# Product with the values ahead of the turn in each attention step, in a two-block transformer kernel

## What is computed

```python
sc = jnp.einsum('bnqgrd,bnkgd->bgrnqk', qb, kk).astype(jnp.float32) * (HEAD_DIM ** -0.5)
sc = jnp.where(mask, sc, NEG)
mx = jnp.maximum(sc.max(axis=-1, keepdims=True), sink)
e = jnp.exp(sc - mx)
p = e / (e.sum(axis=-1, keepdims=True) + jnp.exp(sink - mx))
o = jnp.einsum('bgrnqk,bnkgd->bnqgrd', p.astype(vv.dtype), vv)
```

## Time and profile before

| | us |
|---|---|
| median of 3 runs | 2529.38 |
| lowest and highest | 2527.14, 2529.92 |
| the profiled execution | 2531.64 |
| its span | 2529.8 |

### The profile page before, as it was taken

The page is one execution under the profiler, slowest core; times in us unless marked ns, Lnnn a source line. Parts: engine busy times, 40 slices in busy tenths (PEclk is TensorE's granted clock), DMA queues, the critical chain, the costliest instruction groups (busy, mean ns, idle before and its releaser), DMA issues.

```text
span 2529.8 us, 30118 instructions
## 1 busy us (share of the span) xinstructions
PE 2370.3 (94%) x11732; PEld 1867.3 (74%) x11732; DVE 1318.5 (52%) x1529; ACT 957.7 (38%) x1392; POOL 280.9 (11%) x188
## 2 busy tenths in 40 slices
PE   7999999999998989999998999999996689999997
PEld 6775667888876667888886678888875547788886
DVE  6447656664545656664647653333365565443333
ACT  3327753442322543442423533232225353332221
POOL 0000003110112003110100032110040001311010
PEclk9999999999999999999998999999998789999998
DMA  4211002222222002222232022322221101222231
GB/s 174 100 67 34 2 18 83 100 99 86 97 98 94 34 34 85 98 99 100 83 110 99 34 83 90 110 91 92 100 86 56 50 1 67 84 100 98 87 114 67
DMA packets 31202, 202.53 MB, mean 80 GB/s; under 512 B 4356, under 2 KB 5256, under 8 KB 7432
## 3 DMA queue, kind: packets, MB, share of 16 engines
q1 hardware_dynamic: 29816, 198.14, 22.2%
q10 hardware_dynamic: 1296, 3.15, 0.3%
HBM read 199.17 MB, written 2.10 MB: 80 GB/s over the span
## 4 chain that ended last, share of the span: by engine, by line
PE 83%; DVE 11%; ACT 4%; issue 1%; DMA 0%; ACTq 0%; DVEq 0%; SPq 0%
PE D L526 71%; PE X L600 3%; PE D L621 2%; PE D L613 2%; DVE neg_max L1680 2%; DVE w_lo L1475 1%; DVE xg L1509 1%; ACT prob L1177 1%; PE X L605 1%; ACT w_hi L1003 1%; DVE mid L1475 1%; DVE prob L1695 1%; ACT mid L1003 1%; PE X L717 1%; PE X L566 1%
## 5 line engine op out<-in xcount | busy, mean ns | idle before, releaser
L526 PE MATMUL D<-xg,w_hi 128*128 128x512 f32 x3184 | 1000.3, 396 | 57.1 <-DVE xg L1509 33.7
L526 PEld LDWEIGHTS D<-xg,w_hi 128*128 128x128 f32 x3184 | 604.4, 191 | 191.0 <-DVE w_lo L1475 25.7
L526 PE MATMUL D<-mid,w_hi 128*128 128x512 f32 x2312 | 719.2, 392 | 15.8 <-DVE w_lo L1475 7.7
L1475 DVE TENSOR_TENSOR w_lo<-w_raw,w_hi 128x2048 fp32r<-128x2048 f32 (+1 forms) x208 | 454.2, 2185 | 375.2 <-ACT w_hi L1003 374.9
L526 PE MATMUL D<-xg,w_lo 128*128 128x512 f32 x1592 | 626.3, 393 | 0.0
L1003 ACT ACTIVATE w_hi<-w_raw 128x2048 fp32r<-128x2048 f32 (+1 forms) x208 | 356.5, 1714 | 476.5 <-PE D L526 474.7
L526 PEld LDWEIGHTS D<-mid,w_hi 128*128 128x128 f32 x2312 | 436.3, 189 | 112.8 <-issue 17.6
L526 PE MATMUL D<-mid,w_lo 128*128 128x512 f32 x1156 | 452.2, 391 | 0.0
L526 PEld LDWEIGHTS D<-xg,w_lo 128*128 128x128 f32 x1592 | 303.3, 190 | 64.1
L526 PEld LDWEIGHTS D<-mid,w_lo 128*128 128x128 f32 x1156 | 218.7, 189 | 45.9
L1524 DVE TENSOR_TENSOR h<-D,h 128x1024 f32 (+1 forms) x72 | 88.0, 1222 | 267.8 <-PE D L526 267.8
(11 more groups left out here) (241 smaller groups left out, 1711.6 us busy)
## 6 DMA issues: line engine op xcount, KB each, us to landing
w_raw<-in_weights SPq DMA_DIRECT2D x184, 1024.0 KB, 4.8
h<-in_x SPq DMA_DIRECT2D x4, 512.0 KB, 7.9
out_y<-h SPq DMA_DIRECT2D x4, 512.0 KB, 2.7
inv_cnt<-in_inv_cnt ACTq DMA_DIRECT2D x1, 1024.0 KB, 4.9
cos<-in_cos ACTq DMA_DIRECT2D x3, 256.0 KB, 4.9
sin<-in_sin ACTq DMA_DIRECT2D x3, 256.0 KB, 5.3
vec<-in_vec SPq DMA_DIRECT2D x1, 262.0 KB, 3.0
cos<-in_cos_m ACTq DMA_DIRECT2D x1, 256.0 KB, 2.9
```

Source lines behind the costliest of these rows:

```text
L526: last = nc.tensor.matmul(out, w[a], x[b], start=start and k == 0, stop=stop and k == 2)
L1475: return nc.vector.tensor_tensor(out, x, f(high), ALU.subtract)
```

## The change

In TensorE's `attend` the block of the product (unit s-3) is moved ahead of the block of the turn (unit s-2). Both keep their waits: the product waits for the copy of its own unit, the turn for the norm of its own unit and for the copy of the unit before, which the product has now already waited for. In nsa the compressed product moves with the product. The two turns of the compressed branch stay where they were, before both.

```diff
-                    if 0 <= s - 2 < count:
-                        n = s - 2
-                        pe.wait_ge(normed, a0 + n + 1)
-                        if n >= 1:
-
-                            pe.wait_ge(evac, a0 + n)
...
-                        turn(kind, units[n], a0 + n)
                     if 0 <= s - 3 < count:
                         n = s - 3
                         t = n // per
...
                         pe.wait_ge(evac, a0 + n + 1)
                         times_values(kind, units[n], a0 + n, n % per == per - 1)
+                    if 0 <= s - 2 < count:
+                        n = s - 2
+                        pe.wait_ge(normed, a0 + n + 1)
+                        if n >= 1:
+
+                            pe.wait_ge(evac, a0 + n)
...
+                        turn(kind, units[n], a0 + n)
```

More of the change, by code:

```diff
@@ L685, in attend @@
                         compressed_turn(g, D[:, 3, :])
+                    if 0 <= s - 3 < count:
+                        n = s - 3
+                        t = n // per
+                        if n % per == 0:
+                            if t >= 2:
+                                pe.wait_ge(ao_low, tiles_before[l] + t - 1)
+                            if kind == "nsa":
+                                pe.wait_ge(c_evac, 4 if t % 2 else t // 2 + 1)
+                                compressed_values(t)
+                        pe.wait_ge(evac, a0 + n + 1)
+                        times_values(kind, units[n], a0 + n, n % per == per - 1)
                     if 0 <= s - 2 < count:
@@ L699, in attend @@
                         turn(kind, units[n], a0 + n)
[L700 to L711, removed]
             def swap(u, out):
```

## The result

| | before | after |
|---|---|---|
| median, us | 2529.65 (4 runs) | 2559.39 (4 runs) |
| lowest and highest | 2527.14, 2531.88 | 2554.65, 2563.93 |
| the profiled execution | 2531.64 | 2558.12 |
| its span | 2529.8 | 2556.3 |

The ratio is 1.0118, 95% interval 1.0103 to 1.0133. The changed kernel is slower, as forecast, but by 29.7 us where I had 10.0, and outside my range (2532.5 to 2546.0).

A forecast was written before the change was run, and what follows sets the result against it. TensorE was taken to set the pace in nsa and odd, a cycle through VectorE in swa. Nsa 5.1 + swa 2.6 + even 1.3 + odd 1.0 = +10.0 us on 2529.4 gave 2539.4, range 2532.5 to 2546.

The forecast's parts named there:

- The bare copies: Settled nsa tile: three products wait for copies longer than the scores covering them, 0.42, 0.63 and 0.42 us.
- three restarts of 0.05 us: Settled nsa tile: each of three products starting from a stop was counted 0.05 us longer.
- The sum by the Trainium skill: Nsa: weight loads pulled ahead make restarts free, so the sum would be 7 x 0.15 = 1.05 us lower.
- Would the norms be late for something else?: Nsa: one product more covers norm waits of at most 0.48 us, except in the first two tiles.
- Nothing is added or removed: Whole change: same matmuls, DMAs and waits, other four queues unchanged; only two waits change places.
- Swa and even: Product ahead of the tile's second turn: 0.37 us at seven swa places, +2.6; 0.45 at three even places, +1.3.
- Odd: Odd layer: scores cover the copy, so nothing in the middle; last product 1.0 us later in the tail, +1.0.
- Rival D, the clock: New nsa stops lower the granted clock once a tile, 14 us on top: 2553; chance 0.09.
- +5.1: Nsa together, in us: 4.6 for seven tiles, +1.2 for the last tile, -0.7 for the first step.
- The ends: Nsa's last tile: no scores left to cover copies, last product +1.6 us, less a 0.38 wait: +1.2.
- The chance of 0.82 for slower: Whole kernel: probability 0.82 of slower, against 0.12 within and 0.06 faster by over 0.2% (5 us).

The follow-up runs named there:

- sink_all: New order of product and turn only in the two sink layers, swa and even, against the kernel before: 2540.23 us against 2528.5, ratio 1.0047.
- nsa_all: New order of product and turn only in the nsa layer, against the kernel before: 2544.6 us against 2530.19, ratio 1.0072.

## Why the prediction was wrong in size

**The bare copies: right.** 0.42, 0.63 and 0.42 us were forecast; the trace has 0.42, 0.63 and 0.43. The three restarts of 0.05 us that I added are not there: the product behind the stop takes 1.02 us (303.04 to 304.06), what it took without one. Its weight load still starts with it at 303.04, not ahead, but so does the load of a product that waits for nothing (294.77 and 294.78), so a stop takes nothing from it. The 0.05 us that I read off a turn behind a stop match the head start of its load behind the masks, which a product never had. The sum by the Trainium skill ("TensorE: Matmul & The Clock Gate", "Step-by-step: what each phase is for"), 1.05 us lower, was the better one in this term, though no load was pulled ahead of the wait.

**"Would the norms be late for something else?": the step that failed first.** I compared the extra product with the norm waits that stood there before, and said that they are covered. I did not follow the moved turn on to who waits for it: ScalarE's copy, then the output copy on ScalarE's queue, then VectorE's low part, then the next norm. I even wrote this chain down for swa and did not ask for it in nsa, where the turn of the second unit gets two products ahead of it. +0.70 us in each settled tile, about 5 us, by the ledger and by the tile of the changed kernel with the late low part.

**"Nothing is added or removed": the second.** The same matmuls in another order are not the same work. One more change of form in each step with masks: +0.89 us a tile in nsa, about 6 us, and it reaches swa and even. That both kernels without masks have the same step, and that the step is back at 2.75 us with the masks next to the turn, shows the price; that it is the form and nothing else in that neighbourhood is argued.

**Swa and even: the mechanism right, the terms short.** The tile's second scores now stop 1.28 us instead of 0.83:

```profile
934.62 0.70 PE L600 MATMUL X<-kd,q_all 64*128 64x256 f32 x4 [1.28 <-DVE X L1661]
```

The step with the stop is 0.49 us longer (2.79 to 3.28), of which 0.37 was forecast for the product ahead of the turn. The rest is the dearer step: the turn ends (the next scores start) 1.28 us behind its masks (930.06 to 931.34) where it ended 0.76 behind them (904.47 to 905.23), 0.52 later, that is 0.37 for the product, 0.09 more from the masks to it and 0.06 more for the turn. The other three steps add 0.15, 0.03 and 0.03: 0.70 a tile. In even the step with the stop is 0.59 longer (3.77 to 4.36) where I had 0.45, and the one behind it 0.14. With seven and three tiles that is 7.1 us against my 3.9, and sink_all measured 11.7.

**Odd: right.** +0.6 where I had +1.0. There are no masks in it, and the step went from 3.82 us (2061.08 to 2064.90) to 3.77 (2083.21 to 2086.98). The number of changes of form is the same in both, so the order of equal numbers of changes can still be worth 0.05 us.

**Rival D, the clock: partly, and in another place.** I had weighed it in nsa's middle, where nothing happened, and held swa's clock of 1.00 against it. In the changed kernel the layer swa lost its clock behind longer stops, and so did the layer even (0.57 over 1480 to 1484 us). Window (columns as in the earlier trace rows), then the step:

```profile
904.00:908.00 4.00, 3.95 (x20) 2.23 (x20) 3.19 (x10) 0.82 (x5) 0.00 (x0) 0.50 0.02 4
```

```profile
904.05 1.23 PE L600 MATMUL X<-kd,q_all 64*128 64x256 f32 x4 [1.88 <-DVE X L1661]
...
907.84 1.23 PE L600 MATMUL X<-kd,q_all 64*128 64x256 f32 x4
...
910.95 0.70 PE L600 MATMUL X<-kd,q_all 64*128 64x256 f32 x4
```

Behind a stop of 1.88 us the clock was at half (1.2 GHz), and two steps took 3.79 and 3.11 us instead of 2.13 and 1.92, +2.9. In sink_all there are three such places in swa, at 0.57, 0.57 and 0.58 over 4 us, one of them at a stop of 1.28 us. Its swa is 9.3 us longer than before where the spacings give 4.9, which fills most of the 4.6 us between its 11.7 and the 7.1 of the spacings. But the execution of nsa_all, whose swa has the old order, also shows 0.95 over 850 to 950 us, and the two kernels with the late low part 0.98. So the granted clock varies from one execution to the next, and how much of it belongs to the change stays open.

The same is so at nsa's start, where it has nothing to do with nsa's order. Over 194 to 206 us, in stretches of 4, the clock was 0.50, 0.50 and 0.76 in the changed kernel and 0.50, 0.50 and 0.78 in sink_all, whose nsa has the old order; in nsa_all, whose nsa has the new one, it was 1.00 throughout. The first tile (compressed product to compressed product) takes 25.32 us in the changed kernel and 21.98 in nsa_all, 3.3 us for the clock alone. The kernel before had 0.57 in one of the three stretches, and nsa (first scores to output projection) takes 167.2 us there and 169.4 in sink_all. So about 2 of nsa's +17.5 in the profiled executions are not the order's.

Nsa's measured 14.4 and the spacings of the other layers (swa 4.9, even 2.2, odd 0.6) make 22.1 us. Of the 26.5 of the profiled executions 4.4 are not in them: the low clock adds 2.1 at nsa's start, 2.9 in swa and 1.6 in even, and the layers between give back 3.0, which leaves 0.8. Of the medians' 29.7 us 7.6 are not in them, or 4 if nsa is taken by its ratio (18); there the clock is the only candidate that the rows show, and no run isolates it.

**Sum.** nsa +14.4 measured by the medians (+18 by the ratio) for +5.1: 4.9 from the chain through `mid`, 6.2 from the changes of form, less 1.05 for the restarts, 10.1 together for the missing 9.3 (13 by the ratio). The ends were mis-sized too: in nsa_all the stretch behind the last compressed product is 2.95 us longer (22.30 for 19.35) where I had +1.2, since the chain and the changes of form reach that tile as well, while the first two tiles together bring 2.3 and not 4.2, at unequal clocks. Swa and even +11.7 for +3.9. Odd as said. The chance of 0.82 for slower was well placed, but the range stood on the assumptions that the order of equal work is free and that no norm comes late for another reason.

## What to carry to other kernels

When a block is moved behind another on one engine, follow its result through each in-order queue until it comes back to the first engine, with every instruction that stands behind the one that waits; the one that waits for a far-off result (here the low part of `mid`) is the first candidate to be issued one step later. On TensorE, count the changes of tile form in a step before and after; here it paid to keep the one pair of equal form together. And a product that fills a wait for norms is no gain if the copy it depends on then has only the short scores to lie under.

## What the runs showed of the hardware

- The neighbour's tile form has a price even with no wait: the masks (two matmuls) cost 0.08 us in a step when a turn of the same form follows, 0.22 when a product of another form does; in the old order removing all masks saves 0.61 us a tile (19.62 to 19.01). The load of the turn begins 0.07 us behind the masks and 0.05 ahead of its matmul, that of the product 0.21 behind them and with its matmul.
- A wait at the head of VectorE's queue of 2.02 us for one copy cost TensorE 0.63 us in nsa, behind a reduction and a norm, and moving the instruction that waited (the low part of `mid`) by a unit was worth 10.4 us in the kernel before.
- The granted clock differed between executions with the same order: in swa 0.98 before and 0.95 in nsa_all (850 to 950 us), at nsa's start 0.50 to 0.76 in the changed kernel and 1.00 in nsa_all. In swa stops of 1.3 to 1.9 us stood at the low stretches of the changed kernel and of sink_all; stops of the same length without a fall stand there too (1.89 us at 894.20, then a step of the full clock's 2.14).
